# Stacked sample products, finish first in the turns, and fp32r dummy products in attention, recurrence and samples of a hybrid decoder trunk

## The reference

```
for l in range(DEPTH):
    x = layer_norm(DN_ALPHA * x + 0.5 * swiglu(x, ffn1_w_in[l], ffn1_w_out[l]), ...)
    f_r, f_s, f_g = jnp.split(x @ w_in[l], ...)
    mix = concatenate([rwkv7_mixer(f_r), swa(f_s), gdn_mixer(f_g)]) @ w_out[l]
    x = layer_norm(DN_ALPHA * x + mix, ...)
    x = layer_norm(DN_ALPHA * x + 0.5 * swiglu(x, ffn2_w_in[l], ffn2_w_out[l]), ...)
```

```
rwkv7, 4 heads:  sa = S @ -kk;  S = S*w + sa (x) (kk*a) + v (x) k;  y = S @ r     per token
swa, 8 q heads, 2 kv heads: softmax over a window of 128 with sinks and a relative bias
gdn, 4 heads:    chunked delta rule, a unit lower triangular A solved per chunk, then
                 u = u_b - w_s @ S;  o = q_n @ S + qk_n @ u;  S = dec*S + k_n.T @ u
```

## Time and profile before

| | |
|---|---|
| median of 3 runs | 3163.85 us (3157.62 to 3167.18) |
| the profiled execution | 3179.77 us, span 3178.0 us |
| mean granted TensorE clock | 0.878 |
| TensorE busy | 2759.1 us, 87% of the span |
| VectorE busy | 1646.1 us, 52% |
| ScalarE busy | 936.7 us, 29% |
| GpSimd busy | 179.6 us, 6% |
| chain that ended last | TensorE 80%, VectorE 10%, ScalarE 4%, issue 4% |
| products of line 622 in the chain | 59% of the span |
| products of line 681 in the chain | 18% |

### The profile page before, as it was taken

One profiled execution on the slowest core, in us unless ns is written; L12 is line 12 of the kernel. 1 busy time (PEld: TensorE's weight loads), 2 busy tenths in 40 slices (PEclk: granted clock), 3 DMA queues, 4 the chain that ended last, 5 costly groups with the idle time before them and its releaser, 6 DMA issues.

```text
span 3178.0 us, 59305 instructions
## 1 busy us (share of the span) xinstructions
PE 2759.1 (87%) x23248; PEld 2577.5 (81%) x23248; DVE 1646.1 (52%) x2431; ACT 936.7 (29%) x1655; POOL 179.6 (6%) x186
## 2 busy tenths in 40 slices
PE   8999999457876799999999999983587878999995
PEld 8999999336654699999999999972465657999995
DVE  5665345345455446663366643543455452566533
ACT  4333233222112233332233322332222121433322
POOL 1030100000000020001100011000000001100011
PEclk9999999766766699999999999996676666999997
DMA  4842343000000123223222232520000002222231
GB/s 106 108 90 83 90 130 111 7 0 5 9 1 8 56 76 88 86 86 89 78 86 86 86 87 85 134 80 2 4 2 8 9 8 79 80 86 86 85 90 46
DMA packets 381421, 201.32 MB, mean 63 GB/s; under 512 B 41381, under 2 KB 378789, under 8 KB 380472
## 3 DMA queue, kind: packets, MB, share of 16 engines
q1 hardware_dynamic: 378872, 197.46, 21.8%
q0 software_dynamic: 2400, 1.82, 1.8%
HBM read 188.07 MB, written 13.34 MB: 63 GB/s over the span
## 4 chain that ended last, share of the span: by engine, by line
PE 80%; DVE 10%; ACT 4%; issue 4%; SPq 1%; DMA 1%; DVEq 0%; ACTq 0%; POOLq 0%; POOL 0%
PE ps L622 59%; PE ps L681 18%; DVE ar L1707 3%; DVE ar L1701 3%; ACT ar L1264 2%; PE ps L724 1%; PE ps L969 1%; PE ps L874 1%; SPq L485 1%; DVE ar L1734 1%; DVE wl L1557 0%; DMA raws<-in_ffn_w_in 0%; ACT wh L1177 0%; DVE x L1701 0%; DVE xl L1701 0%
## 5 line engine op out<-in xcount | busy, mean ns | idle before, releaser
L622 PE MATMUL ps<-xh,wh 128*128 128x272 f32 x3776 | 795.6, 292 | 44.0 <-DVE xl L1701 17.9
L1557 DVE TENSOR_TENSOR wl<-raws,wh 128x1024 fp32r<-128x1024 f32 x332 | 406.6, 1225 | 752.5 <-ACT wh L1177 748.6
L622 PE MATMUL ps<-xh,wl 128*128 128x272 f32 x3776 | 788.3, 290 | 0.0
L622 PE MATMUL ps<-xl,wh 128*128 128x272 f32 x3776 | 786.5, 290 | 0.0
L681 PE MATMUL ps<-ar 64*64 64x64 f32 (+14 forms) x4984 | 505.4, 299 | 167.7 <-DVE ar L1704 45.9
L622 PEld LDWEIGHTS ps<-xh,wh 128*128 128x128 f32 x3776 | 602.2, 191 | 50.8 <-issue 26.5
L622 PEld LDWEIGHTS ps<-xl,wh 128*128 128x128 f32 x3776 | 602.6, 191 | 0.0
L681 PEld LDWEIGHTS ps<-ar 64*64 64x64 f32 (+6 forms) x4984 | 379.7, 181 | 274.1 <-issue 68.0
L622 PEld LDWEIGHTS ps<-xh,wl 128*128 128x128 f32 x3776 | 601.5, 191 | 0.0
L1177 ACT ACTIVATE wh<-raws 128x1024 fp32r<-128x1024 f32 x332 | 350.7, 1057 | 472.1 <-PE ps L622 454.8
L622 PE MATMUL ps<-hh,wh 128*128 128x272 f32 x1408 | 292.2, 289 | 0.0
(11 more groups left out here) (179 smaller groups left out, 2296.5 us busy)
## 6 DMA issues: line engine op xcount, KB each, us to landing
raws<-in_ffn_w_in SPq DMA_DIRECT2D x176, 512.0 KB, 3.8
raws<-in_ffn_w_out SPq DMA_DIRECT2D x64, 512.0 KB, 3.7
raws<-in_w_in SPq DMA_DIRECT2D x42, 512.0 KB, 3.6
raws<-in_ffn_w_out SPq DMA_DIRECT2D x32, 384.0 KB, 3.4
raws<-in_w_out SPq DMA_DIRECT2D x16, 512.0 KB, 3.7
x_kept<-x SPq DMA_DIRECT2D x2, 2176.0 KB, 10.9
x<-x_kept SPq DMA_DIRECT2D x2, 2176.0 KB, 8.0
ar<-in_consts SPq DMA_DIRECT2D x2, 1337.5 KB
```

The costliest lines, as they stand in the source:

```text
L622: ins = pe.matmul(ps[:, bank + h, 0:n1 - h * NH], w[u % 2][:, k, :], a[:, k0 + k, h * NH:n1], start=(first and k == 0 and n == 0), stop=(l ...
L1557: dve.tensor_tensor(wl[u % 2][:, :, :], raw[u % 2][:, :, :], wh[u % 2][:, :, :].bitcast(F32), ALU.subtract).then_inc(sem("wl_done"), 1)
```

## The change

Four things change.

1. `alternate`: a step k of finish stands at k/n instead of (k + 1)/n and goes first in a tie. All engines' queues change with it.
2. rwkv samples: the two products of 32 rows and 512 columns for each half become one of 64 rows. `mb` holds the masked rows of both tensors one above the other, for each half of the pair in its own 64 partitions (four VectorE products of 32x512 instead of two of 32x1024), and a new tile `uv` holds us above the values (four new ScalarE copies, semaphore `uv_copied`).
3. `keep_busy(bank, n)` now runs for all pairs and in attention: 48 products before each tile's transposes and 8 behind them; 20 at the start of each recurrence (behind the waits for the pair's inverse, ahead of the one for `head_l`); three behind cu and three behind cy of each tile; three at the start of the samples and behind each of sz, sx, su and sy; three at the head norm's start. Those ahead of cx and of the cu wait in pair 3, and its eight ahead of the norm, go.
4. Two waits move: in attention `probs` now stands behind the waits for `kts`, `pt_v` and `pt_a` and behind the 48 products; in the samples `m_next`, the recurrence's last state, is waited for at the start instead of ahead of sy.

```diff
 def alternate(first, n_first, second, n_second):
-    order = sorted([((k + 1) / n_first, 0) for k in range(n_first)] + [((k + 1) / n_second, 1) for k in range(n_second)])
-    for _, which in order:
+    order = sorted([((k + 1) / n_first, 1, 0) for k in range(n_first)] + [(k / n_second, 0, 1) for k in range(n_second)])
+    for _, _, which in order:
         next((first, second)[which])
...
+                def keep_busy(bank, n):
+                    for _ in range(n):
+                        pe.matmul(ps[:, bank, 0:NH], xh[:, 0, 0:P], xh[:, 7, 0:NH], start=True, stop=True)
...
-                    pe.wait_ge(sem("probs"), at(lay, "probs", n + 1))
                     if n == 0:
...
                         pe.wait_ge(sem("pt_a"), at(lay, "pt_a", n - 1))
+                    keep_busy(7, 48)
+                    pe.wait_ge(sem("probs"), at(lay, "probs", n + 1))
...
                     ins.then_inc(*tick("probs_t"))
+                    keep_busy(2, 8)
...
-                def keep_busy(p, n):
-                    if p.q == 3:
-                        for _ in range(n):
-                            pe.matmul(ps[:, 3, 0:NH], xh[:, 2, 0:P], xh[:, 3, 0:NH], start=True, stop=True)
...
                     pe.wait_ge(sem("inv_a"), at(lay, "inv_a", N_INV_A * (q + 1)))
                     pe.sem_inc(passed, 1)
+                    keep_busy(3, 20)
...
-                            keep_busy(p, 3)
                             pe.wait_ge(sem("m_next"), at(lay, "m_next", 4 * q + i))
...
                         ins.then_inc(*tick("cu"))
+                        keep_busy(4, 3)
                         yield
-                        keep_busy(p, 3)
                         pe.wait_ge(sem("cu_copied"), at(lay, "cu_copied", 4 * q + i + 1))
...
                         ins.then_inc(*tick("cy"))
+                        keep_busy(4, 3)
...
                             for b in range(DEC_BATCH):
                                 mm(ps[pr, 7, b * HD:(b + 1) * HD], s0[pr, b, :], p.dg[pr, b, :], ...)
-                            mm(ps[pr, 7, :], us[0:NSAMP, hc], p.mb[:, :, hc], ...)
-                            ins = mm(ps[pr, 7, :], tok[0:NSAMP, 4, 2, hc], p.mk[:, :, hc], ...)
+                            ins = mm(ps[pr, 7, :], p.uv[pr, :], p.mb[pr, :, :], ...)
...
-                    keep_busy(p, 8)
+                    keep_busy(5, 3)
...
+                    if not gd:
+                        for hp in range(2):
+                            hc = slice(hp * HD, (hp + 1) * HD)
+                            go(p.uv[64 * hp:64 * hp + NSAMP, :], ps[0:NSAMP, 5, hc]).then_inc(*tick("uv_copied"))
+                            go(p.uv[64 * hp + NSAMP:64 * hp + 2 * NSAMP, :], p.tok[0:NSAMP, 4, 2, hc]).then_inc(*tick("uv_copied"))
```

More of the change, by code:

```diff
@@ L427, in __init__ @@
                     a = KH * NT
-                    self.s0, self.mb = self.over(a, 512), self.over(a + 512, 1024, NSAMP)
-                    self.mk, self.dg = self.over(a + 1536, 1024, NSAMP), self.over(a + 2560, 512)
+                    self.s0 = self.over(a, 512)
+                    self.mb, self.uv, self.dg = self.over(a + 512, 512), self.over(a + 1536, HD), self.over(a + 2560, 512)
                     self.us, self.so, self.zs = self.over(a + 3072, P), self.over(a + 3200, 512), self.over(a + 3712, NSAMP)
@@ L434, in __init__ @@
                 if not self.gd:
-                    self.mk, self.dg = (t.rearrange("p (b n) -> p b n", b=DEC_BATCH) for t in (self.mk, self.dg))
+                    self.dg = self.dg.rearrange("p (b n) -> p b n", b=DEC_BATCH)
             def over(self, o, w, rows=P):
@@ L1034, in samples @@
                     pe.sem_inc(passed, 1)
+                    pe.wait_ge(sem("m_next"), at(lay, "m_next", 4 * (q + 1)))
+                    pe.sem_inc(passed, 1)
+                    keep_busy(6, 3)
                     if not gd:
@@ L1089, in samples @@
                                 mm(ps[pr, 7, b * HD:(b + 1) * HD], s0[pr, b, :], p.dg[pr, b, :], start=(b == 0), stop=False, skip_group_check=True)
-                            mm(ps[pr, 7, :], us[0:NSAMP, hc], p.mb[:, :, hc], start=False, stop=False, skip_group_check=True)
-                            ins = mm(ps[pr, 7, :], tok[0:NSAMP, 4, 2, hc], p.mk[:, :, hc], start=False, skip_group_check=True)
+                            ins = mm(ps[pr, 7, :], p.uv[pr, :], p.mb[pr, :, :], start=False, skip_group_check=True)
                     ins.then_inc(*tick("s_fin"))
@@ L2064, in samples @@
                     else:
-                        for dst, s in ((p.mb, 0), (p.mk, 1)):
-                            tt(dst, bc(tok[0:NSAMP, 4, s, :].rearrange("p (o n) -> p o n", o=1), [NSAMP, DEC_BATCH, P]), bc(rm, [NSAMP, DEC_BATCH, P]), ALU.mult).then_inc(*tick("d_seq"))
+                        for hp in range(2):
+                            for s in range(2):
+                                o = 64 * hp + NSAMP * s
+                                tt(p.mb[o:o + NSAMP], bc(tok[0:NSAMP, 4, s, hp * HD:(hp + 1) * HD].rearrange("p (o n) -> p o n", o=1), [NSAMP, DEC_BATCH, HD]),
+                                   bc(rm, [NSAMP, DEC_BATCH, HD]), ALU.mult).then_inc(*tick("d_seq"))
                     yield
```

10 lines of the change are left out of this document (5 added, 5 removed).

## The result

The changed kernel takes 3176.15 us (median of 7 runs, 3171.24 to 3182.26), the kernel before 3162.84 us in the same runs: ratio 1.0048, 95% interval [1.0034, 1.0062]. It is slower by 0.5%. Forecast were 3138 us and faster; the time lies within the range of 3090 to 3195.

What follows compares the result with a forecast made beforehand. It took TensorE itself, at 1.2 GHz for 54% to 72% of the paired stretches, as mostly the bound; terms +2.4 - 10 + 36 + 5 + 5 + 2 - 10.6 - 56 = -26 off median 3163.85 gave 3138 us, range 3090 to 3195.

Steps and rivals of the forecast that it cites:

- Turns: Finish steps first at each pair's end: inverse's copies 3.0 us late, pair 1 wins 3 us; +2.4 a layer, +5.
- Stacked products: Samples in pairs 0 and 1: each half loses one 512-column product; 2.6 us per pair, four pairs, -10.6 us.
- All dummies with what the clock gives back: Attention's dummies +2.4, groups of three +36, bursts +5, pair 3 +2, faster attention products -10, half of 112 us returned -56.
- rival B: Mixing part: the dummies cost their time, 33 groups a layer on the path, and lift nothing; +44, 3208 us; 28%.
- Bursts and pair 3: 20 dummies at each finish's start cost 2.5 us in pair 0, twice, +5; more groups in pair 3 alone, +2.
- rival A: TensorE at full clock throughout: all 112 us, full attention gain and pair 3's 18 us twice; 3032 us; 8%.
- full clock for the attention products: Sign of being right: attention products behind the eight dummies take 2.0 us in nearly all tiles.
- slow transposes: Sign of being right, in attention: transposes still take 3.7 us, as the 48 dummies end 6.5 us before them.
- the 512-column pair gone: Sign of being right, in the samples: the pair of 512-column products no longer appears.
- Attention's part: Attention in both layers: dummies cost +2.4 us; six attention and score products, 1.7 us each, won by full clock, -10.
- the forecast's case: Half of the 112 us in the paired stretches given back, -56; 3138 us, own range 3105 to 3154; 52%.
- C: Wash: the clock gives back 26 to 35 us, time within 0.3% (9.5 us) of before; 12%.

Runs made afterwards that it cites:

- Stacked only: The kernel before with the stacked sample products alone: 3144.82 us, ratio 0.9936.
- after, old turns, no bursts: The changed kernel with the turns of before and without the 20 dummies at each finish's start: 3142.89 us, ratio 0.9933.
- after, old turns: The changed kernel with the turns of before, the 20 dummies at each finish's start writing bank 7 instead of 3: 3145.23 us, ratio 0.9952.
- first trace of before: The first profiled execution of the kernel before, unchanged: 3179.77 us, 16 us above its median.
- second trace of before: A second profiled execution of the kernel before, unchanged: 3158.79 us; that series' median 3159.44 us, ratio 1.0001.

## Why the prediction was wrong

**Turns, priced +5, measured +31.** This is the step that failed, the largest of two. Its local part was right: the inverse's copies were to be 3.0 us late and are 3.1. Wrong was that I counted only waits at the pairs' ends and no clock, that I let pair 1 win 3 us (its 6.09 us wait of VectorE moved on to the next copy, 5.70 us), and that I took the burst before it at full clock (2.5 us; it takes 4.87). The runs show losses that no wait in my sum held. The two end steps cost 17 us alone: the inverse's last products now run at half clock between two waits (1.94 us instead of 1.13). The earlier steps of recurrence and samples cost 8 us alone with no more waiting. Alone, the turns added 32.5 us of real work and 2.0 of idle; in the changed kernel without bursts 22.6 and 13.2. That the earlier steps put their waits where TensorE was about to regain full clock fits the windows above, but is argued, not shown, since the old turns have the same slow stretch in some executions.

**Stacked products, priced -10.6, measured -20** (0.9936). The mechanism was right, the size was not: I took 2.6 us a pair, and the rows by form give 15.6 us over four pairs. The rest is not separated from the clock.

**All dummies with what the clock gives back, priced 2.4 + 36 + 5 + 2 - 10 - 56 = -21, measured 0 to -2.** This is the second step that failed. "Stacked only" and "after, old turns, no bursts" differ by the dummies, their profiles lie at their medians, and their times agree (0.9936 and 0.9933). The give-back came, 53.7 us of TensorE's real time, against 56 and 10 in attention; so rival B's "lift nothing" is wrong, though the time came out on its side of the kernel before. The cost was more than I took: dummy time rises by 130.5 us and idle falls by 78.0, which leaves 52.5 us on the path against some 40 (45 less 5 for the bursts). With the bursts ("after, old turns", whose profile is 14 us faster than its median) the same columns give 80 and 67 us, and the timed runs again nothing (0.9952). With bursts in all pairs and groups in pair 3 alone the real time is already 49 us below stacked alone (2644.0); the groups in pairs 0 to 2, 252 dummies, add 64 us of dummy time and lift 31 us more at most.

**Bursts and pair 3, priced +5 and +2 and no gain; the burst before pair 3 is worth -24.** I read 0.52 at 37 us of work in 43 as proof that dummies can't lift the clock there, and used it against rival A. The row shows a clock that was lost in the 4.42 us wait ahead of it and not regained; it does not tell what happens if the stretch starts at full clock. Here A had the direction: TensorE works 11.65 us less in the stretch, of A's 18. Without the burst the new groups cost 3 us a layer there (50.2 us instead of 47.3), against +2 for both.

**Right:** full clock for the attention products, slow transposes in seven of eight tiles, whatever the dummies before them, the 512-column pair gone. Attention's part was right in size as well: its stage is 3.0 and 4.9 us shorter with its dummies alone, against -10 and +2.4 forecast. Pair 0's stretch is 7.7 and 1.5 us shorter (163.5 and 169.6 against 171.2 and 171.1), but it took 180.4 us in layer 0 of the first trace of before, so this shows nothing. The changes add up by medians from kernel to kernel: stacked -18, dummies 0, turns +31, from 3163 to 3176. The forecast differs by 26 us of turns and 21 of dummies, less 8 of stacking. That 3176 lies inside 3090 to 3195 is owed to the width of that range: the forecast's case and those of B and C each rest on another give-back and cheaper turns.

Not settled is what part of the give-back belongs to which group, why the same queue takes 105 us for pair 1's stretch in one execution and 110 in another, and why the clock returns later with the new turns: that TensorE works at half clock longer is shown, what on the chip decides it was not tested.

## What to carry to other kernels

Where TensorE's clock falls in short waits, find the wait behind which a long stretch runs slow, and fill that wait; here it paid with a few small groups behind it. Dummies spread over a busy stretch cost more than they lifted. Before moving steps between two interleaved streams, compare TensorE's busy time at an equal number of instructions, not only its waits: here one step earlier lost 27 us with 2 us more of waiting, and half a step later lost 34 us, 28 of it by waiting. Read a mechanism of the clock from more than one trace of a kernel: two of before differ by 24 us of TensorE's work. Time a change of many parts part by part: one part of this one gained 20 us, one lost 31, and 40 of its 944 dummies, one burst of 20 in each layer, brought what the dummies did in the best kernels here (its 0.72% and stacking's 0.64% make 1.36%; the best have 1.34 to 1.37%).

## What was unexpected in the hardware

A long run of busy time at half clock did not bring the clock back, and a short dense burst did. In the second trace of before, TensorE works without a gap behind the wait before pair 3, on small products with the groups of three between, and stays at 0.50:

```profile
1055.00:1076.00 21.00, 21.00 (x94) 14.91 (x94) 2.54 (x9) 0.83 (x3) 0.00 (x0) 0.50 0.22 92
```

With the burst in that wait 1.09 us of it are left, and the next 37 us run at 0.76 in the mean (the groups of three take 0.62 us instead of 1.02). The burst does so from half clock too: in the changed kernel it stands behind two waits, starts at 0.50, takes 4.52 us instead of 2.77, and the clock is 1.00 from some 1071 to 1089 us. It matters what stands behind the burst, and how much of a wait is left: without groups the clock fell again within 4 us in one layer, and after attention's 48 dummies 6.18 us were left and the transposes were slow. The length of what is left does not decide it alone: in tile 0 of attention 2.15 us were left in layer 0 and the eight transposes took 1.94 us, half clock, and 3.30 us in layer 1, where they took 1.09, full clock.

The Trainium skill, "TensorE: Matmul & The Clock Gate", in its part on the clock gate, calls the slow state the default, which activity releases. The return to full clock by 904 us in before agrees, and so does the burst; pair 3 in before, where TensorE worked 37.39 of 48.6 us and the clock stayed at 0.54, does not.
